# Masked score blocks of a chunked recurrence: one product per level instead of one merged product per half

## The chip, the cores and the metric

The kernel runs on one core of one Trainium2 chip. Its time is the device time of one launch in microseconds. The engines are named as the profile names them: PE is TensorE's matmul row and PEld its weight loads, DVE is VectorE, ACT is ScalarE, POOL is GpSimd and SP is SyncE, whose queue here only issues DMAs.

## The reference

The reference is a two-layer hybrid block followed by one more block of another kind. The change lies in one branch of the two layers, a gated linear recurrence over 512 latent tokens and 256 context tokens, which the reference computes by chunks of 64 tokens, for four heads of width 64 and in two directions (d = 0 forwards, d = 1 backwards):

```python
def step(state, inp):                     # one chunk of 64 tokens
    qc, kc, vc, lf = inp
    a = jnp.cumsum(lf, axis=2)
    ...
    inter = jnp.einsum("bhtk,bhkv->bhtv", qc * jnp.exp(a), state)
    diff = a[:, :, :, None, :] - a[:, :, None, :, :]
    dec = jnp.exp(jnp.where(causal, diff, -jnp.inf))
    scores = jnp.einsum("bhtk,bhsk,bhtsk->bhts", qc, kc, dec)
    intra = jnp.einsum("bhts,bhsv->bhtv", scores, vc)
    return s_new, inter + intra
```

The output of a layer is the sum of both directions. In layer 0 all 768 tokens are computed, in layer 1 the recurrence gives an output for the 512 latent tokens only. Everything else (projections, attention, Fourier mixing, convolution, the second block with its delta rule, cross attention and feed-forward part) is the same before and after.

## The kernel before

Features lie on the 128 partitions, tokens along the free dimension. A projection of layer `ly` is 28 output tiles of 128 features; each tile is summed over eight blocks k of the contraction, and each block takes three fp32r matmuls for a piece of 512 columns (leading part of the weights times leading part of the input, and two products with the remainders) and in layer 0 three more for a piece of 256 columns. `project_split` (L1751) issues them. The first 16 tiles alternate between the two halves of `wide_ps`. From tile 16 on all tiles use half 0 alone, so PE waits at every tile's end until ACT has copied the tile out (L687).

The recurrence runs inside tiles 16 to 27: after each of the 96 blocks of these 12 tiles ("slots" 0 to 95, eight to a tile) `project_split` calls `recurrent_piece(ly, slot)`, which may put a group of small fp32 matmuls into PE's queue. The order of all engines is thus written out by hand. The two head pairs j = 0 and j = 1 come one after the other; the second begins at the slot `SECOND`.

The decay inside a chunk isn't formed. The kernel works by levels l = 0 to 5 with blocks of b = 2^l tokens: at a level the queries of one half of each block of 2b tokens meet the keys of the other half, and between levels DVE multiplies queries and keys by the gates of the block just closed. For each level and direction:

- PE, `scores` (L1892): for each chunk of 128 tokens four matmuls of 64 rows by 64 columns with 32 moving columns, one in each quadrant of the array, from `hg_k` and half of the columns of `hg_q` into `score_bank(d, r)`. Direction 0 has the two banks of `wide_ps[:, 1]`, direction 1 the two of `pair_ps`. That is 24 matmuls in layer 0 (six chunks) and 16 in layer 1 (four); each appears twice in the profile, so a group is 48 or 32 records.
- DVE, `level` (L1210 to L1216): two predicated copies (one for each head of the pair) put the wanted elements of the score banks into one tile `pair_scores`, which the kernel had cleared before (L1367); then one multiplication of the queries (L1213), one of the keys (L1214) and one of the gates (L1216). The two directions write to different elements of `pair_scores`.

The score groups of both directions are issued together, at slots 3, 7, 11, 15, 19 and 23 of the pair. When all twelve are merged, `values` (L1904) multiplies `pair_scores` by the values once, with 64 moving columns, into `pair_ps` (`out_bank`). `keys_by_token` (L1848) turns the keys at slot 26, ACT copies them (L743), `updates` (L1870) forms the state increments of both directions at slot 31, in `duo_ps` and in `wide_ps[:, 1]`, DVE's `states` (L1227, L1231) runs the recurrence over 12 chunks, and `carried` (L1917) adds the part that comes from the states at slot 39. `head_mean` (L1942) sums squares for a head's norm; ACT's `head_root` follows it with a logarithm and an exponential, each set with its own table load, before it copies out the next tile.

With `SECOND = 48` the groups at slots 7, 15, 23, 31, 39, 47, 55, 63, 71, 79, 87 and 95 stand between the last block of a tile and the first of the next.

POOL subtracts the leading part from each weight chunk (L528, 128x1024 elements) soon after ACT has written that part (L700), once for each tile, and multiplies queries and keys for the diagonal (L567, L569).

Of the kernel before, what the change touches and what calls it, by code (L numbers as in the profile page):

```python
# [22 lines left out]
P = 128  # L23
# [119 lines left out]
def build(nc, tokens, mem, positions, weights, const_d, const2_d, par_d, out):  # L143
    with ExitStack() as ctx:
# [44 lines left out]
        pair_scores = proj[:, CV, :].rearrange("p (r t) -> p r t", r=2)  # L189
# [12 lines left out]
        two_banks = lambda d: (wide_ps[:, 1, :], pair_ps[:, :])[d]  # L202
        score_bank = lambda d, r: two_banks(d)[:, 512 * r:512 * r + 512]
        update_ps = lambda d: (duo_ps[:, :], wide_ps[:, 1, :])[d]
# [422 lines left out]
        def _(act):  # L627
# [111 lines left out]
            def keys_by_token(ly, j, d):  # L739

                u = 4 * ly + 2 * j + d
                act.wait_ge(hg_kt_ps, u + 1)
                act.activation(k_tok(d), update_ps(d)[:, 0:TOK].rearrange("p (c f) -> p c f", c=NCH), ACT.Copy).then_inc(hg_kt, 1)  # L743
# [36 lines left out]
            def recurrent_steps(ly, t):  # L780
# [11 lines left out]
                if t == 21:  # L792
                    act.wait_ge(hg_s, 4 * ly + 2)
                    for d in range(2):
                        gates(ly, 1, d)
                if t == 22:
                    values_by_token(ly, 1)
# [3 lines left out]
                if t == 25:  # L801
                    for d in range(2):
                        keys_by_token(ly, 1, d)
                if t == 26:
                    act.wait_ge(sc_used, 2 * ly + 2)
# [322 lines left out]
        def _(dve):  # L1128
# [58 lines left out]
            def level(ly, j, l):  # L1187
# [3 lines left out]
                for d in range(2):  # L1191
# [14 lines left out]
                    mask = cst[f"level{d}"][:, 32 * l:32 * l + 32].bitcast(I32).rearrange("p (n b) -> p n b", b=b)  # L1206
                    mask = mask.unsqueeze(1).broadcast_to([P, len(chunk_list(ly)), HD // (2 * b), b])
                    for r in range(2):
                        mine_of = halves(pair_scores[:, r, 0:2 * cols], b)[:, :, mine, :].rearrange("p (c n) b -> p c n b", c=len(chunk_list(ly)))
                        ins = dve.copy_predicated(mine_of, mask, score_bank(d, r)[:, 0:cols].rearrange("p (c n b) -> p c n b", b=b, n=HD // (2 * b)))  # L1210
# [9 lines left out]
            def states(ly, j, d):  # L1220
# [3 lines left out]
                new = lambda c: update_ps(d)[:, 512 * (c % 2) + 64 * (c // 2):512 * (c % 2) + 64 * (c // 2) + 64]  # L1224
# [132 lines left out]
            for ly in range(DEPTH):  # L1357
# [8 lines left out]
                dve.wait_ge(conv_out, 2 * ly)  # L1366
                link(dve.memset(proj[:, CV, :], 0.0))  # L1367
# [1264 lines left out]
```

## Time and profile before

| | |
|---|---|
| median of 3 runs | 1953.26 us (1952.07 to 1955.52) |
| profiled execution | 1953.26 us, span of the engines 1951.5 us |
| mean granted TensorE clock | 0.964 |
| PE busy, PEld busy | 1766.4 us (91%), 1405.0 us (72%) |
| DVE, ACT, POOL busy | 812.1 us (42%), 717.0 us (37%), 598.2 us (31%) |
| chain that ended last | PE 41%, DVE 7%, ACT 2%, issue 2% of the span |

Busy shares are of the whole span. A busy PE isn't a PE at its peak, since the ends of matmuls are modelled; the distance between the starts of two matmuls tells more than their durations, which contain the way through the array. The granted clock is 1 at full speed (2.4 GHz) and 0.50 at half (1.2 GHz).

### The profile page before, as it was taken

What the parts mean: (1) busy time and instruction counts of PE and PEld (TensorE: products, weight loads), DVE (VectorE), ACT (ScalarE), POOL (GpSimd) and SP (SyncE); (2) the same over time, 40 slices, a digit from 0 to 9 for tenths busy, and PEclk for the clock granted to TensorE, in tenths of its full rate; (3) what the DMA queues carried; (4) which work ended last, traced back from release to release, by engine and by line L of the source; (5) the groups of instructions that cost most, each with busy time, mean ns of one, the idle gap of its engine ahead of it and who ended that gap; (6) DMA issues with size and microseconds to landing.
All of it is one profiled execution on the core that took longest, in us unless ns stands there. A gap on an engine that the chain in (4) does not pass through costs nothing.

```text
span 1951.5 us, 32357 instructions
## 1 busy us (share of the span) xinstructions
PE 1766.4 (91%) x13594; PEld 1405.0 (72%) x13594; DVE 812.1 (42%) x1471; ACT 717.0 (37%) x1115; POOL 598.2 (31%) x318
## 2 busy tenths in 40 slices
PE   6799899978989988989879988888999999999996
PEld 2687788845878766657767766887678678888885
DVE  0301165417350265355656658656424443323112
ACT  3323413226343624254543877003433432222222
POOL 0221312173113323453013411311334334444442
PEclk9899999999999999999899999899999999999998
DMA  8344311130122111311422210000220222222231
GB/s 324 103 158 142 108 35 45 62 113 1 45 86 86 65 56 55 109 44 65 140 99 86 86 55 2 3 3 12 76 76 22 76 76 91 93 98 97 97 107 66
DMA packets 43145, 154.27 MB, mean 79 GB/s; under 512 B 4480, under 2 KB 5632, under 8 KB 42752
## 3 DMA queue, kind: packets, MB, share of 16 engines
q1 hardware_dynamic: 39456, 142.82, 21.2%
q10 hardware_dynamic: 3552, 9.44, 1.3%
q8 instruction: 108, 1.77, 0.4%
q14 instruction: 29, 0.24, 0.0%
HBM read 148.05 MB, written 4.19 MB: 78 GB/s over the span
## 4 chain that ended last, share of the span: by engine, by line
PE 41%; DVE 7%; ACT 2%; issue 2%; DVEq 0%; ACTq 0%
PE wide_ps L1751 29%; PE wide_ps L1772 2%; PE pair_ps L2327 1%; PE wide_ps L2324 1%; PE wide_ps L2303 1%; PE wide_ps L2262 1%; DVE xn L1519 1%; PE duo_ps L2431 1%; PE wide_ps L2412 1%; DVE xn L1669 1%; PE wide_ps L1787 1%; PE pair_ps L1826 1%; DVE ring_r L1170 1%; PE pair_ps L2262 0%; DVE h L1673 0%
## 5 line engine op out<-in xcount | busy, mean ns | idle before, releaser
L528 POOL TENSOR_TENSOR ring_r<-ring,scratch_r 128x1024 fp32r<-128x1024 f32 x179 | 432.2, 2415 | 1082.8 <-ACT scratch_r L700 1054.8
L1751 PE MATMUL wide_ps<-xn_r,scratch_r 128*128 128x512 f32 (+1 forms) x1320 | 490.1, 371 | 0.0
L1751 PE MATMUL wide_ps<-work_r,scratch_r 128*128 128x512 f32 (+1 forms) x1151 | 445.2, 387 | 22.9 <-DVE xn_r L1162 12.0
L700 ACT ACTIVATE scratch_r<-ring 128x1024 fp32r<-128x1024 f32 x195 | 206.7, 1061 | 609.7 <-PE wide_ps L1751 456.8
L1751 PE MATMUL wide_ps<-work_r,ring_r 128*128 128x512 f32 (+1 forms) x1151 | 429.5, 373 | 0.0
L1751 PEld LDWEIGHTS wide_ps<-xn_r,scratch_r 128*128 128x128 f32 x1320 | 252.1, 191 | 49.1 <-issue 5.4
L1751 PEld LDWEIGHTS wide_ps<-work_r,scratch_r 128*128 128x128 f32 x1151 | 218.7, 190 | 75.0 <-issue 18.8
L1751 PEld LDWEIGHTS wide_ps<-work_r,ring_r 128*128 128x128 f32 x1151 | 218.8, 190 | 40.0
L1751 PE MATMUL wide_ps<-proj_r,scratch_r 128*128 128x512 f32 x704 | 238.0, 386 | 1.5 <-DVE proj_r L1162 1.5
L1751 PEld LDWEIGHTS wide_ps<-proj_r,scratch_r 128*128 128x128 f32 x704 | 133.1, 189 | 31.1 <-DVE proj_r L1162 1.9
L687 ACT ACTIVATE proj<-wide_ps 128x512 f32<-128x512 f32 (+2 forms) x116 | 73.8, 636 | 163.8 <-PE wide_ps L1751 154.8
L1267 DVE SCALAR_TENSOR_TENSOR proj<-proj,par_sb,qe 128x768 f32<-128x768 f32 (+1 forms) x6 | 6.2, 1037 | 213.2 <-ACT qe L651 213.2
L1315 DVE TENSOR_TENSOR work<-work 128x512 f32<-128x512 f32 (+2 forms) x35 | 36.4, 1041 | 125.0 <-ACT work L659 124.2
L1751 PE MATMUL wide_ps<-proj_r,ring_r 128*128 128x512 f32 x208 | 82.6, 397 | 0.0
L1751 PE MATMUL wide_ps<-conv_tmp_r,scratch_r 128*128 128x512 f32 (+1 forms) x185 | 69.4, 375 | 0.0
L1751 PE MATMUL wide_ps<-conv_tmp_r,ring_r 128*128 128x512 f32 (+1 forms) x185 | 69.2, 374 | 0.0
L1703 DVE TENSOR_TENSOR proj<-proj,qe 128x512 f32<-128x512 f32 x11 | 27.5, 2501 | 82.2 <-ACT qe L687 82.2
L1703 DVE TENSOR_TENSOR proj<-proj,state 128x512 f32<-128x512 f32 x11 | 27.5, 2500 | 80.5 <-ACT state L687 80.5
L1335 DVE TENSOR_TENSOR h<-h,work 128x768 f32<-128x768 f32 (+1 forms) x16 | 29.8, 1862 | 65.3 <-ACT work L871 65.3
L659 ACT ACTIVATE work<-h 128x512 f32<-128x512 f32 (+2 forms) x56 | 36.2, 660 | 54.2 <-DVE work L1315 16.6
L1751 PEld LDWEIGHTS wide_ps<-proj_r,ring_r 128*128 128x128 f32 x208 | 39.3, 189 | 9.3
L2016 PE MATMUL wide_ps<-proj 64*128 64x256 f32 (+1 forms) x144 | 29.7, 529 | 17.1 <-ACT xn L827 14.5
(392 smaller groups left out, 2906.4 us busy)
## 6 DMA issues: line engine op xcount, KB each, us to landing
ring<-weights SPq DMA_DIRECT2D x260, 512.0 KB, 3.5
h<-tokens SPq DMA_DIRECT2D x4, 768.0 KB, 11.8
h<-tokens ACTq DMA_DIRECT2D x1, 3072.0 KB, 10.0
out<-h ACTq DMA_DIRECT2D x1, 2048.0 KB, 7.3
h<-out ACTq DMA_DIRECT2D x1, 2048.0 KB, 8.6
out<-h SPq DMA_DIRECT2D x8, 256.0 KB, 2.1
const_sb<-const SPq DMA_DIRECT2D x1, 1089.0 KB, 6.3
h<-mem ACTq DMA_DIRECT2D x1, 1024.0 KB, 12.1
```

Source lines behind the costliest of these rows:

```text
L528: pool.tensor_tensor(as_r(wt), wt, as_r(w_lead(m)).bitcast(F32), ALU.subtract).then_inc(w_split, 1)
L659: act.activation(square_sum(n)[:, 0:w] if first else squares(n)[:, k % 2, 0:w], src, ACT.Square).then_inc(sq_ready, 1)
L687: act.activation(dst, wide_ps[0:rows, g % 2 if bank is None else bank, 0:w], func).then_inc(evacuated, 1)
L700: act.activation(as_r(w_lead(m)), ring[:, c % RING, :], ACT.Copy).then_inc(w_lead_ready, 1)
L1170: dve.tensor_tensor(as_r(wt), wt, as_r(w_lead(m)).bitcast(F32), ALU.subtract).then_inc(w_split, 1)
L1315: dve.tensor_tensor(total, total, squares(n)[:, k % 2, 0:w], ALU.add).then_inc(sq_used, 2 if k == 1 else 1)
L1335: dve.tensor_tensor(h[:, n, 0:w], h[:, n, 0:w], resid[:, n % 2, 0:w], ALU.add).then_inc(h_ready, 1)
L1519: link(dve.tensor_tensor_reduce(probs(n)[:, r * (b - a):(r + 1) * (b - a)], win_bank(n, r)[:, 0:b - a], cst2["window"][:, ma:mb], HD ** -0 ...
L1703: dve.tensor_tensor(tile_2[:, t, :], tile_2[:, t, :], up_2[t % 2], ALU.mult).then_inc(ffn_ready, 1)
L1751: last = pe.matmul(wide_ps[:, bank, a:b], wt[:, cols], as_r(x[:, a:b]), start=n == 0 and p == 0, stop=n == len(k_order) - 1 and p == 2)
L1772: last = pe.matmul(ps[:, a:b], wt[:, cols], as_r(x[:, a:b]), start=k == 0 and p == 0, stop=k == KT - 1 and p == 2)
L2016: last = pe.matmul(wide_ps[:, r, a:b], proj[rows, AQ + i, c * CH:(c + 1) * CH], proj[rows, AK, a:b], start=True, stop=True)
```

## The change

The merge is given up. Each level and direction gets its own masked block, and PE multiplies each of them by the values.

- DVE multiplies the score bank by a 0/1 mask (`tensor_tensor`, one operand in PSUM, one in SBUF) into `masked(l, d)`, one of four places in two of the 28 projection tiles, in place of the predicated copy. The clearing of the merged tile goes. Before it writes, DVE waits until the values product of four groups earlier has been done.
- PE's `values` is issued for each level and direction: 12 groups for each pair and layer in place of one, with 32 moving columns, written to every second run of b columns of the output bank.
- Both directions use one pair of score banks, so the scores of one direction wait for the masking of the other's. The output bank is then free for the whole time.
- Both directions' state increments use `duo_ps`; `updates(1)` waits for `states(0)`.
- The slots are laid out anew: scores at 1 and 2, then scores and values in turn at each slot from 4 to 23, the diagonal at 6, keys at 24 and 28, the last values at 25 and 26, updates at 30 and 35, `carried` at 40, and `SECOND` is 46. `head_mean` of the first pair is at slot 60 (before 62) and of the second at 93 (before 95). ACT's copies follow this order.

```diff
-        pair_scores = proj[:, CV, :].rearrange("p (r t) -> p r t", r=2)
+        masked = lambda l, d: proj[:, CV + d, 384 * (l % 2):384 * (l % 2) + 384].rearrange("p (r t) -> p r t", r=2)
...
-        score_bank = lambda d, r: two_banks(d)[:, 512 * r:512 * r + 512]
-        update_ps = lambda d: (duo_ps[:, :], wide_ps[:, 1, :])[d]
+        score_bank = lambda r: wide_ps[:, 1, 512 * r:512 * r + 512]
...
-                    if e > 1:
-                        dve.wait_ge(sc_ready, e - 1)
-                    if l == 0 and d == 0:
-                        dve.wait_ge(sc_used, 2 * ly + j)
+                    if e > 4:
+                        dve.wait_ge(sc_used, e - 4)
...
-                        ins = dve.copy_predicated(mine_of, mask, score_bank(d, r)[:, 0:cols].rearrange("p (c n b) -> p c n b", b=b, n=HD // (2 * b)))
+                        ins = dve.tensor_tensor(masked(l, d)[:, r, 0:cols].rearrange("p (c t) -> p c t", t=32),
+                                                score_bank(r)[:, 0:cols].rearrange("p (c t) -> p c t", t=32), mask, ALU.mult)
...
-                dve.wait_ge(conv_out, 2 * ly)
-                link(dve.memset(proj[:, CV, :], 0.0))
...
             def updates(ly, j, d):
-                pe.wait_ge(hg_kt, u + 1)
+                pe.wait_ge(hg_kt, 4 * ly + 2 * j + 2)
+                if d:
+                    pe.wait_ge(hg_s, u)
...
             def scores(ly, j, l, d):
-                if e > 2:
-                    pe.wait_ge(sc_ready, e - 2)
+                if e > 1:
+                    pe.wait_ge(sc_ready, e - 1)
...
-            def values(ly, j):
-                pe.wait_ge(sc_ready, level_count(ly, j, HG_LEVELS - 1, 1))
+            def values(ly, j, l, d):
+                e = level_count(ly, j, l, d)
+                pe.wait_ge(sc_ready, e)
...
-                            last = pe.matmul(out_bank(a)[rows, 64 * c:64 * c + 64], hg_v[tokens_half, c, rows],
-                                             pair_scores[tokens_half, r, 64 * c:64 * c + 64], start=c == 0, stop=False, skip_group_check=True)
+                            last = pe.matmul(halves(out_bank(a)[rows, 64 * c:64 * c + 64], 1 << l)[:, :, 1 - d, :], hg_v[tokens_half, c, rows],
+                                             masked(l, d)[tokens_half, r, 32 * c:32 * c + 32], start=l == 0 and d == 0 and c == 0,
+                                             stop=False, skip_group_check=True)
...
-            SECOND = 48
+            SECOND = 46
...
-                if slot in (0, SECOND - 1):
+                if n == 0:
                     heads_by_token(ly, j)
-                if 3 <= n < 24 and n % 4 == 3:
-                    for d in range(2):
-                        scores(ly, j, n // 4, d)
+                if n in (1, 2):
+                    scores(ly, j, 0, n - 1)
+                if 4 <= n < 24:
+                    l, step = divmod(n - 4, 4)
+                    d, of_values = divmod(step, 2)
+                    if of_values:
+                        values(ly, j, l, d)
+                    else:
+                        scores(ly, j, l + 1, d)
...
-                if n == 31:
-                    for d in range(2):
-                        updates(ly, j, d)
-                if n == 39:
+                if n == 24:
+                    keys_by_token(ly, j, 0)
+                if n in (25, 26):
+                    values(ly, j, HG_LEVELS - 1, n - 25)
+                if n == 28:
+                    keys_by_token(ly, j, 1)
+                if n in (30, 35):
+                    updates(ly, j, (n - 30) // 5)
+                if n == 40:
                     carried(ly, j)
```

## Rows read from the trace of the kernel before

**Rows 1.** Busy time by stretch: both recurrence stretches, then two pieces at half clock.

```profile
core 0: us, PE busy (x) PEld busy (x) DVE busy (x) ACT busy (x) POOL busy (x), PEclk, DMA share, GB/s
241.00:396.00 155.00, 148.45 (x2252) 128.72 (x2252) 78.92 (x172) 37.32 (x42) 32.53 (x14) 0.97 0.18 63
697.00:816.00 119.00, 104.62 (x1492) 81.38 (x1492) 67.21 (x172) 39.78 (x48) 32.18 (x15) 0.97 0.22 74
346.00:351.80 5.80, 5.80 (x18) 4.93 (x19) 4.18 (x3) 0.95 (x1) 2.37 (x1) 0.50 0.00 0
778.60:781.90 3.30, 3.30 (x9) 2.27 (x7) 0.09 (x1) 0.00 (x0) 2.37 (x1) 0.50 0.00 0
```

**Rows 2.** Waits of PE, whole run: total us, times, longest us.

```profile
PE pair_ps L1892 <- DVE proj L1214: 5.1, 5, 1.5
PE wide_ps L1848 <- DVE proj L1214: 4.5, 4, 1.5
```

**Rows 3.** Waits of PE in the two stretches alone, layer 0 first.

```profile
PE wide_ps L1751 <- ACT proj L687: 4.5, 3, 2.7
...
PE wide_ps L1751 <- ACT proj L687: 6.3, 3, 2.9
```

**Rows 4.** Timeline of PE, layer 0, a pair of score groups (start, duration, what).

```profile
247.93 0.28 PE L1751 MATMUL wide_ps<-work_r,ring_r 128*128 128x256 f32 x1
248.14 0.90 PE L1892 MATMUL wide_ps<-h,proj 64*64 64x32 f32 x48
248.86 0.88 PE L1892 MATMUL pair_ps<-h,proj 64*64 64x32 f32 x48
249.67 0.50 PE L1751 MATMUL wide_ps<-work_r,scratch_r 128*128 128x512 f32 x1
250.01 0.39 PE L1751 MATMUL wide_ps<-xn_r,scratch_r 128*128 128x512 f32 x1
250.24 0.39 PE L1751 MATMUL wide_ps<-work_r,ring_r 128*128 128x512 f32 x1
```

**Rows 5.** Timeline of PE, layer 0, the single group of values.

```profile
287.76 0.28 PE L1751 MATMUL wide_ps<-work_r,ring_r 128*128 128x256 f32 x1
287.97 0.93 PE L1904 MATMUL pair_ps<-proj,h 64*64 64x64 f32 x48
288.83 0.50 PE L1751 MATMUL wide_ps<-work_r,scratch_r 128*128 128x512 f32 x1
```

**Rows 6.** Timeline of PE, layer 1, a pair of score groups.

```profile
757.68 0.40 PE L1751 MATMUL wide_ps<-work_r,ring_r 128*128 128x512 f32 x1
758.01 0.67 PE L1892 MATMUL wide_ps<-h,proj 64*64 64x32 f32 x32
758.50 0.65 PE L1892 MATMUL pair_ps<-h,proj 64*64 64x32 f32 x32
759.07 0.50 PE L1751 MATMUL wide_ps<-work_r,scratch_r 128*128 128x512 f32 x1
```

**Rows 7.** Timelines at tile ends: PE and ACT in layer 0, ACT in layer 1.

```profile
315.07 0.82 PE L1848 MATMUL duo_ps<-const_sb,proj 128*128 128x128 f32 x6
316.13 0.50 PE L1751 MATMUL wide_ps<-work_r,scratch_r 128*128 128x512 f32 x1 [0.24 <-ACT proj L687]
...
315.26 0.81 ACT L687 ACTIVATE proj<-wide_ps 128x768 f32<-128x768 f32 x1 [5.59 <-PE wide_ps L1751]
...
744.39 0.60 ACT L687 ACTIVATE proj<-wide_ps 128x512 f32<-128x512 f32 x1 [5.63 <-PE wide_ps L1751]
```

**Rows 8.** Timelines of DVE and POOL, layer 0: two places where they overlap.

```profile
257.43 2.56 POOL L528 TENSOR_TENSOR ring_r<-ring,scratch_r 128x1024 fp32r<-128x1024 f32 x1 [14.23 <-ACT scratch_r L700]
...
257.65 2.76 DVE L1214 TENSOR_TENSOR proj<-proj,h 128x384 f32<-128x384 f32 x1
...
294.45 3.13 DVE L1231 SCALAR_TENSOR_TENSOR state<-state,h,duo_ps 128x64 f32<-128x64 f32 x10
...
295.28 2.40 POOL L528 TENSOR_TENSOR ring_r<-ring,scratch_r 128x1024 fp32r<-128x1024 f32 x1 [10.72 <-ACT scratch_r L700]
```

**Rows 9.** Busy time in a later stretch of 64x64 matmuls alone, columns as Rows 1.

```profile
1251.00:1290.00 39.00, 39.00 (x1344) 39.00 (x1341) 20.25 (x42) 0.00 (x0) 0.00 (x0) 1.00 0.02 5
```

More of the change, by code:

```diff
@@ L1855, in keys_by_token @@
                 if d:
[L1856 removed]
+                    pe.wait_ge(hg_kt, u)
                 elif j:
@@ L1869, in updates @@
                         for r, rows in enumerate(HALF):
-                            last = pe.matmul(update_ps(d)[rows, 512 * a + 64 * c:512 * a + 64 * c + 64], k_tok(d)[tokens_half, c, rows],
+                            last = pe.matmul(duo_ps[rows, 512 * a + 64 * c:512 * a + 64 * c + 64], k_tok(d)[tokens_half, c, rows],
                                              hg_v[tokens_half, c, rows], start=True, stop=True, skip_group_check=True)
@@ L1891, in scores @@
                         for r, rows in enumerate(HALF):
-                            last = pe.matmul(score_bank(d, r)[tokens_half, 32 * c:32 * c + 32], hg_k(j, d)[rows, chunk_cols(c, a)],
+                            last = pe.matmul(score_bank(r)[tokens_half, 32 * c:32 * c + 32], hg_k(j, d)[rows, chunk_cols(c, a)],
                                              halves(hg_q(d)[rows, chunk_cols(c, a)], 1 << l)[:, :, 1 - d, :], start=True, stop=True,
@@ L1952, in heads_by_token @@
                 by_token(proj[:, HI[j], :], duo_ps, vt_ps)
-            SECOND = 48
+            SECOND = 46
             def recurrent_piece(ly, slot):
-                j, n = (0, slot) if slot < SECOND - 1 else (1, slot - SECOND)
-                if slot in (0, SECOND - 1):
+                j, n = (0, slot) if slot < SECOND else (1, slot - SECOND)
+                if n == 0:
                     heads_by_token(ly, j)
-                if 3 <= n < 24 and n % 4 == 3:
-                    for d in range(2):
-                        scores(ly, j, n // 4, d)
-                if n == 5:
-                    diagonal(ly, j)
-                if n == 26:
-                    for d in range(2):
-                        keys_by_token(ly, j, d)
-                if n == 27:
-                    values(ly, j)
-                if n == 31:
-                    for d in range(2):
-                        updates(ly, j, d)
-                if n == 39:
+                if n in (1, 2):
[7 more added lines that the diff above has]
+                        scores(ly, j, l + 1, d)
+                if n == 6:
+                    diagonal(ly, j)
+                if n == 24:
[7 more added lines that the diff above has]
+                if n == 40:
                     carried(ly, j)
@@ L1977, in recurrent_piece @@
                     head_mean(ly, 0)
-                if slot == 95:
+                if slot == 93:
                     head_mean(ly, 1)
```

28 lines of the change are left out of this document (12 added, 16 removed).

## The prediction

> **What bounds the kernel now.** I read the shares of busy time first, then the waits of PE, then PE's timeline through the two stretches in which the recurrence runs. In those stretches PE is busy for 148.45 of 155 us in layer 0 and for 104.62 of 119 us in layer 1, DVE for 78.92 and 67.21 us [rows 1]. The projection's matmuls follow each other at 0.23 us for 512 columns [rows 4], and half of that, 0.12, for 256. Nothing waits for weights there. So PE's in-order queue is the path: whatever is put into it, and whatever it waits for inside it, moves the end of the layer. A slot of the projection is 3 x (0.23 + 0.12) = 1.05 us in layer 0 and 0.69 us in layer 1.
>
> The waits that the change can touch are few. PE waits 9.6 us for DVE's key multiplications in all [rows 2], and the longest wait for ACT's tile copy is 2.7 us in layer 0 and 2.9 us in layer 1 [rows 3]; that is the tile end at which ACT is still busy with the root of the head norm.
>
> **The change part by part.**
>
> *The groups.* In layer 0 the stream before a pair of score groups would have gone on at 247.93 + 0.12 = 248.05; it goes on at 249.67, and its first matmul takes 0.34 until the next start where 0.23 is usual [rows 4]. A pair costs 1.62 + 0.11 = 1.73 us, of which the second group is 0.72. The single group of values costs 288.83 - 287.88 + 0.11 = 1.06 us [rows 5], although it has 64 moving columns where the scores have 32: the spacing, 0.015 us a record, doesn't depend on the columns here. In layer 1 the pair costs 759.07 - 757.91 + 0.11 = 1.27 us, the second group 0.49 of it [rows 6]; a single one is then 0.78, and 0.83 with the 0.05 by which layer 0's measured single exceeds its own difference.
>
> Before, a pair of heads has six score pairs and one values group. After, it has 24 groups, each in a slot of its own. Layer 0: 24 x 1.06 - 6 x 1.73 - 1.06 = 14.0 us. Layer 1: 24 x 0.83 - 6 x 1.27 - 0.83 = 11.5 us. Twice each, for j = 0 and 1: **+50.9 us**. The value groups that the trace doesn't show (32 columns, written to every second run) I price by the nearest row, the score groups, which read such runs. Lower bound: only the spacing of the 44 more groups, 22 x 0.72 + 22 x 0.49 = 26.6 us. Upper bound: the 64x64 matmuls of the later stretch, half of whose products are written so, which take 39.00 us for 1344 records, 0.029 us each [rows 9]; that stretch uses two quadrants at a time where the recurrence uses four, so I don't take it.
>
> What a change of tile shape costs is 1.73 - 2 x 0.72 = 0.29 us, the part of a pair that isn't its groups [rows 4]; 17 more such changes in each of four halves make 19.7 of the 50.9 us. The Trainium skill, TensorEngine Tiling, Key Properties, says that changing the tiling mode drains the engine. By that rule a regrouping into single slots is what one wouldn't do; without it the sum would be 19.7 us lower. The trace agrees with it.
>
> *Updates and keys apart.* Four pairs of update groups (24 matmuls in both layers) become singles: 2 x 1.06 - 1.73 = 0.39 each; with some 0.1 for each of the four pairs of transposes: **+2.0**.
>
> *Tile ends.* Before, a group stands at each tile's end and hides ACT's copy. How much it hides is seen at 315.07: the stream would have gone on there, the copy runs from 315.26 for 0.81 us, and PE goes on at 316.13 [rows 7], 1.06 us later, 1.17 with the slow first matmul. In layer 1 the copy takes 0.60 [rows 7], so 0.96. After the change nothing stands at slots 31, 39, 79 and 87: 4 x 1.17 + 4 x 0.96 = 8.5 us. At seven other tile ends of each layer a single group of 0.95 or 0.72 covers 1.06 or 0.85: 14 x 0.12 = 1.7. Together **+10.2**. The last `head_mean`, which ran beside the last copy, now stands two slots earlier in the open: at most a single group's price in each layer, 1.06 and 0.83, of which I take 0.75 each: **+1.5**.
>
> *Waits that go.* The scores of the two directions now stand two slots apart, each with its values between: 2 x (1.05 + 1.06) = 4.2 us in layer 0, 2 x (0.69 + 0.83) = 3.0 in layer 1. DVE's whole work in the stretch is 78.92 / 24 = 3.3 and 67.21 / 24 = 2.8 us for each level and direction [rows 1], states and all. So the keys are ready when scores need them, and the 9.6 us of [rows 2] go, with about 1.4 us of half clock behind one of them: the granted clock of 0.97 over 119 us means 7 us at half clock in layer 1, of which 3.3 lie elsewhere [rows 1]. `head_mean` is two slots earlier, which with the groups between gives ACT 3 x 1.05 + 3 x 1.06 = 6.3 us before the tile ends where it had 1.05 + 1.73 + 2.7 = 5.5; in layer 1 3 x 0.69 + 3 x 0.83 = 4.6 where it had 0.69 + 1.27 + 2.9 = 4.9. The wait goes in layer 0 (2.7) and all but some 0.5 in layer 1 (2.4). PE then doesn't stand still, and the half clock after it (0.50 over 5.80 and 3.30 us [rows 1]) gives back 2.9 and 1.6. Sum: 9.6 + 1.4 + 2.7 + 2.4 + 2.9 + 1.6 = **-20.6**.
>
> *Waits that come.* With `SECOND` at 46 the scores of the second pair stand at slots 47 and 48, and in layer 1 the gates (ACT, twice as many operations as in layer 0), POOL's products and DVE's mask of level 0 come later than that. What is late next is DVE: its query multiplication has both operands in SBUF, and such an operation took 2.76 us beside POOL's 2.56 us subtraction [rows 8]. PE's next score group waits for the mask behind it. I take one such wait, 2.8 us, and half clock behind it as in [rows 1], 1.6: **+4.4**. Below, nothing, if POOL happens to be idle; above, the same in layer 0 too, 8.8.
>
> *DVE's own saving* (masking by one multiplication, no clearing) I cost at nothing: DVE stands idle for half of the time [rows 1], and it waits for PE. The new mask operation has one operand in PSUM; DVE's state chain, which has too, ran ten operations in 3.13 us straight through POOL's 2.40 us [rows 8], so POOL doesn't hold it up.
>
> Sum: 50.9 + 2.0 + 10.2 + 1.5 - 20.6 + 4.4 = +48.4 us. The profiled execution took 1953.26 us, which is also the median, around a span of 1951.5. **Forecast: 1953.3 + 48.4 = 2001.7 us.** PE has no later wait for something that isn't shifted with it, so nothing absorbs it.
>
> **The rivals.**
>
> 1. *PE waits for masks.* One pair of banks: each score group waits for the masking of the one before. Against it: the 4.2 and 3.0 us above. For it: POOL holds DVE up by more than 2 us once a tile, and layer 1 has 0.2 us of room by my average. If the 44 score groups after the first of each half waited 0.5 us each, +22: 2024 us.
> 2. *The value groups are slower.* At 0.029 us a record a group is 1.40 us instead of 0.72 in layer 0 and 0.93 instead of 0.49 in layer 1: 24 x 0.68 + 24 x 0.44 = +27, so 2029 us. The Trainium skill, TensorE: Matmul & The Clock Gate, Back-to-back issue gap, gives a floor of about 25 ns from start to start however small the matmul. The 0.015 us of [rows 4] are below it, four quadrants at work, so the trace speaks against it.
> 3. *Cheaper regrouping.* Only the spacing is added (26.6 instead of 50.9), the rest as above: 1977 us. It would need the change of shape to cost nothing when it comes at every slot; [rows 4 to 6] show it each time.
> 4. *Other side, faster.* What PE gets back (20.6 us) outweighs what it is given. Place: the 44 value groups. They would have to cost under 20.6 / 44 = 0.47 us each, all else nothing; even their bare spacing is 0.72 and 0.49. At 0.3 us, with no tile end exposed, 13 - 21 = -8: 1945 us.
>
> **How the numbers follow.** Forecast 0.62, rival 1 0.12, rival 2 0.08, rival 3 0.14, rival 4 0.04. The forecast's own range is 1990 to 2013: the waits that come from nothing to 8.8, and half of the 20.6 not returned. Toward rivals 1 and 3 I widen it to 1982 to 2023, which leaves out rival 2, rival 4 and the outer parts of 1 and 3, under 0.2. A difference of under 0.2%, 4 us, is about what a measurement of this kernel can't tell from none. Slower takes all cases but the fourth: 0.95; same 0.02, faster 0.03.
>
> **What the profile of the changed kernel would show.** PE: 24 single groups for each half, value groups of 48 and 32 records spaced 0.015 us, 1.0 and 0.8 us of the stream each (rivals 2 and 3 fall or stand by this). The two stretches longer by some 26 and 22 us, the rest equal. The waits of PE for DVE's L1214 gone, and the wait of 2.7 us for ACT with its half clock too. Gaps of 1 us at four tile ends of each layer. In layer 1 one wait of PE of 2 to 3 us soon after slot 48. DVE's busy time down. Waits of PE's score groups for the mask line would mean rival 1. The forecast fails if the groups hide beside something I haven't seen, or if the clock falls to half more often than now.

## The result, and the profile after

The change makes the kernel slower: a median of 2006.96 us (2000.58 to 2008.24, 4 runs) against 1954.39 us (1952.07 to 1957.18, 4 runs) for the kernel before on the same chip, a ratio of 1.0262 with a 95% interval of 1.0235 to 1.0288. That is about 51 us; the forecast was 48.4, and 2006.96 lies in its range. The profiled execution took 2004.55 us around a span of 2002.8 us, at a mean granted clock of 0.963.

Busy time over the whole span, from the page of the kernel after:

```profile
PE 1819.8 (91%) x15354; PEld 1436.4 (72%) x15354; DVE 798.4 (40%) x1469; ACT 717.4 (36%) x1115; POOL 597.2 (30%) x318
```

PE has 1760 more records (15354 for 13594), which is 22 x 48 + 22 x 32: the 44 added groups. PE is busy 53 us longer, about as much as the span has grown (51). DVE is busy 14 us less, and nothing of that shows in the time.

Busy time by stretch, columns as in [rows 1]: the two recurrence stretches, then a piece of the second one.

```profile
242.00:424.00 182.00, 173.47 (x3308) 147.43 (x3308) 72.51 (x172) 39.72 (x44) 32.93 (x15) 0.99 0.17 57
725.00:864.00 139.00, 128.27 (x2198) 92.34 (x2197) 65.08 (x173) 39.51 (x47) 31.40 (x16) 0.96 0.21 67
795.40:806.60 11.20, 11.19 (x142) 7.34 (x142) 5.43 (x14) 0.00 (x0) 0.00 (x0) 0.54 0.01 1
```

From the first matmul of tile 16 to the first one behind tile 27 (of the Fourier mixing, so that the wait for the last head norm's root is inside), the stretch of layer 0 goes from 157.4 us (241.51 to 398.95) to 182.2 (242.17 to 424.33), and that of layer 1 from 118.9 (697.32 to 816.23) to 139.0 (724.56 to 863.59). They hold 24.7 and 20.1 us of the 51.3 by which the spans differ. The other 6.5 lie before, between and behind them, 3.9 behind the second, where no instruction was changed.

PE's timeline in layer 0, four slots with one group each, the matmuls of the slots between left out:

```profile
265.58 0.28 PE L1743 MATMUL wide_ps<-conv_tmp_r,ring_r 128*128 128x256 f32 x1
265.79 0.90 PE L1883 MATMUL wide_ps<-h,proj 64*64 64x32 f32 x48
266.62 0.50 PE L1743 MATMUL wide_ps<-work_r,scratch_r 128*128 128x512 f32 x1
266.95 0.39 PE L1743 MATMUL wide_ps<-xn_r,scratch_r 128*128 128x512 f32 x1
...
267.86 0.90 PE L1899 MATMUL pair_ps<-proj,h 64*64 64x32 f32 x48
...
269.93 0.90 PE L1883 MATMUL wide_ps<-h,proj 64*64 64x32 f32 x48
...
272.01 0.90 PE L1899 MATMUL pair_ps<-proj,h 64*64 64x32 f32 x48
```

And in layer 1:

```profile
740.39 0.67 PE L1883 MATMUL wide_ps<-h,proj 64*64 64x32 f32 x32
740.99 0.50 PE L1743 MATMUL wide_ps<-work_r,scratch_r 128*128 128x512 f32 x1
...
741.88 0.67 PE L1899 MATMUL pair_ps<-proj,h 64*64 64x32 f32 x32
```

The starts of neighbouring groups are 2.07 us apart in layer 0. The slot itself is 1.05, so a group costs 1.02 us of the stream. In layer 1 they are 1.49 apart, of which 0.69 is the slot: 0.80 us. Value groups (L1899) and score groups (L1883) have the same length and leave the same gap behind them, although the first write to every second run and have other operands.

Waits of PE over the whole run, where the change touches them (total us, times, longest us):

```profile
PE wide_ps L1743 <- ACT proj L685: 11.0, 12, 1.7
PE pair_ps L2056 <- ACT proj L649: 7.5, 2, 4.1
PE wide_ps L1883 <- DVE proj L1203: 3.3, 3, 2.4
```

The 9.6 us of [rows 2] for the multiplied keys are gone. The waits for ACT's tile copy have the same total as before, 10.8 us in 6 then and 11.0 in 12 now, but they are others: the two long ones of [rows 3] have given way to many of 0.7 to 1.0. This is one of those of layer 0, in the PE timeline and in ACT's:

```profile
305.57 0.50 PE L1743 MATMUL wide_ps<-work_r,scratch_r 128*128 128x512 f32 x1
...
307.78 0.50 PE L1743 MATMUL wide_ps<-work_r,scratch_r 128*128 128x512 f32 x1 [0.90 <-ACT proj L685]
```

```profile
306.92 0.81 ACT L685 ACTIVATE proj<-wide_ps 128x768 f32<-128x768 f32 x1 [3.37 <-PE wide_ps L1743]
```

No group stands between the tile's last block and the next tile's first, so PE waits for the whole copy (in [rows 7] a group lies beside it). The slot takes 2.21 us from start to start, 1.16 more than a bare one, although the profile counts only 0.90 as idle: idle time begins at the modelled end of the last matmul, later than the point at which the next could have started. So the waits of the profile are lower bounds of what they cost. The last kind of wait is new. At the start of the second pair in layer 1, PE's timeline (first fence), DVE's and POOL's:

```profile
790.72 0.67 PE L1883 MATMUL wide_ps<-h,proj 64*64 64x32 f32 x32 [0.39 <-DVE proj L1203]
...
795.41 0.95 PE L1883 MATMUL wide_ps<-h,proj 64*64 64x32 f32 x32 [2.43 <-DVE proj L1203]
796.29 0.79 PE L1743 MATMUL wide_ps<-work_r,scratch_r 128*128 128x512 f32 x1
...
797.87 1.08 PE L1899 MATMUL pair_ps<-proj,h 64*64 64x32 f32 x32
```

```profile
790.49 1.15 DVE L1207 TENSOR_TENSOR h<-h 128x256 f32<-128x256 f32 x1
791.55 2.72 DVE L1208 TENSOR_TENSOR proj<-proj,h 128x384 f32<-128x384 f32 x1
```

```profile
791.31 2.55 POOL L526 TENSOR_TENSOR ring_r<-ring,scratch_r 128x1024 fp32r<-128x1024 f32 x1
```

DVE's multiplication of the keys of level 0, direction 0 takes 2.72 us beside POOL's subtraction, where it takes 0.55 alone (545 to 553 ns in the other 47 cases). The mask of direction 1 stands behind it in DVE's order, and the score group of level 1 waits 2.43 us for that mask. Then PE's matmuls are longer (1.08 us for a group of 32 records, 0.67 elsewhere) for 11.2 us, in which the granted clock is 0.54. What that costs can be read off the same layer's first pair, where the same groups run at full clock:

```profile
730.46 0.67 PE L1883 MATMUL wide_ps<-h,proj 64*64 64x32 f32 x32
...
737.42 0.67 PE L1883 MATMUL wide_ps<-h,proj 64*64 64x32 f32 x32
```

From the score group of level 1, direction 0 to that of level 2, direction 0 it is 6.96 us here, of which some 0.15 are a tile's end that the second pair doesn't have, and 11.26 there (795.41 to 806.67): 4.5 us lost.

### The profile page after: what moved, and what is told of

It is laid out like the page before. It is cut to its first block, busy times and chain, and to the rows that moved or that the text cites. A ratio compares the mean times of both kernels' runs of the same rounds, so it can differ in the third digit from the quotient of the medians.

```text
span 2002.8 us, 35872 instructions
## 1 busy us (share of the span) xinstructions
PE 1819.8 (91%) x15354; PEld 1436.4 (72%) x15354; DVE 798.4 (40%) x1469; ACT 717.4 (36%) x1115; POOL 597.2 (30%) x318
## 4 chain that ended last, share of the span: by engine, by line
PE 40%; DVE 6%; ACT 2%; issue 2%; DVEq 0%; ACTq 0%
PE wide_ps L1743 28%; PE wide_ps L1764 2%; PE pair_ps L2329 1%; PE wide_ps L2326 1%; PE wide_ps L2305 1%; PE wide_ps L2264 1%; DVE xn L1511 1%; PE duo_ps L2433 1%; PE wide_ps L2414 1%; DVE xn L1661 1%; PE wide_ps L1779 1%; PE pair_ps L1818 1%; DVE ring_r L1167 1%; PE pair_ps L2264 0%; DVE h L1665 0%
## 5 line engine op out<-in xcount | busy, mean ns | idle before, releaser
L1743 PE MATMUL wide_ps<-work_r,scratch_r 128*128 128x512 f32 (+1 forms) x1151 | 452.7, 393 | 24.1 <-DVE xn_r L1159 12.2
L1743 PEld LDWEIGHTS wide_ps<-xn_r,scratch_r 128*128 128x128 f32 x1320 | 251.0, 190 | 47.6 <-issue 6.2
L1309 DVE TENSOR_TENSOR work<-work 128x512 f32<-128x512 f32 (+2 forms) x35 | 36.4, 1040 | 125.2 <-ACT work L657 124.3
L1203 DVE TENSOR_TENSOR proj<-wide_ps,const_sb 128x192 f32<-128x192 f32 (+1 forms) x96 | 26.6, 319 | 83.1 <-PE wide_ps L1883 81.7
## 6 DMA issues: line engine op xcount, KB each, us to landing
h<-tokens ACTq DMA_DIRECT2D x1, 3072.0 KB, 10.2
```

Of the source, the lines that this page charges most:

```text
L1203: ins = dve.tensor_tensor(masked(l, d)[:, r, 0:cols].rearrange("p (c t) -> p c t", t=32), score_bank(r)[:, 0:cols].rearrange("p (c t) -> p ...
L1309: dve.tensor_tensor(total, total, squares(n)[:, k % 2, 0:w], ALU.add).then_inc(sq_used, 2 if k == 1 else 1)
L1743: last = pe.matmul(wide_ps[:, bank, a:b], wt[:, cols], as_r(x[:, a:b]), start=n == 0 and p == 0, stop=n == len(k_order) - 1 and p == 2)
```

## The experiments

Nine kernels ran. To read the traces against each other I use one measure besides the time: from the start of the first score group to the start of the last `head_mean` group of a layer. These are 92 slots in the kernels with the second pair at 46 and in before and its variants, and 94 in the three with `SECOND` at 48, from which I take two bare slots (2.10 and 1.38 us). The stretches are from the profiled executions, in us, the ratios from all runs of each kernel.

| kernel | layer 0 | layer 1 | ratio to before, 95% interval |
|---|---|---|---|
| before | 146.1 | 111.4 | 1 |
| after | 170.0 | 130.9 | 1.0262 (1.0235 to 1.0288) |
| no_values | 154.7 | 116.9 | 1.0096 (1.0069 to 1.0124) |
| pairs | 163.0 | 119.2 | 1.0176 (1.0158 to 1.0195) |
| second48 | 170.5 | 125.3 | 1.0228 (1.0202 to 1.0253) |
| tile_ends | 165.3 | 126.6 | 1.0209 (1.0190 to 1.0227) |
| pairs_ends | 157.9 | 116.5 | 1.0102 (1.0078 to 1.0126) |
| mask_twice | 171.7 | 128.3 | 1.0263 (1.0246 to 1.0281) |
| before_single | 147.6 | 111.7 | 1.0021 (1.0007 to 1.0036) |
| before_root | 140.6 | 108.2 | 0.9954 (0.9936 to 0.9972) |
| before_root_keys | 138.6 | 106.5 | 0.9940 (0.9921 to 0.9959) |

### The price of the value groups

```diff
-                    if of_values:
-                        values(ly, j, l, d)
-                    else:
+                    if not of_values:
                         scores(ly, j, l + 1, d)
```

(The waits of DVE and ACT that count value groups are adapted, and the first group that is left starts the accumulation.)

> The changed kernel with the value groups of levels 0 to 4 left out: only the two groups of the last level are issued for each pair and layer, so 10 of 12 value groups and with them most of the product of the scores and the values inside a chunk are not computed. Everything else, the masks, the score groups and the slots, stays. Taken out are 20 groups in layer 0 and 20 in layer 1. Theory (value groups cost what the pair in a slot costs, with a change of shape in each): the slot with one group lasts 1.02 us for a value group in layer 0 and 0.80 in layer 1, so -(20 x 1.02 + 20 x 0.80) = -36 us against the changed kernel, about +15 against the kernel before. Rival A (a group costs only its matmuls at the spacing of the scores, 48 x 0.015 = 0.72 and 32 x 0.015 = 0.48): -(14.4 + 9.6) = -24 us. Rival B (matmuls of a value group are slower, 0.029 us each): about -(20 x 1.4 + 20 x 0.93) = -47 us or more.

Measured: 1971.29 us against 1952.28, a ratio of 1.0096. Against the changed kernel that is 0.0166 of 1952, or 32 us less, between the 36 of the theory and the 24 of rival A; the value groups slower than the scores (rival B) are out. The waits decide between the other two. Some of the value groups stood at tile ends, and without them ACT's copies are exposed there:

```profile
PE wide_ps L1743 <- ACT proj L685: 19.8, 21, 1.8
```

That is 8.8 us more in 9 more waits than in the kernel after. The theory's 36.4 less 8.8 make 27.6, and by the table the two stretches shrank by 15.3 + 14.0 = 29.3; rival A would leave 24 - 8.8 = 15. The cleanest piece is layer 0 up to the first `head_mean`, at full clock in both kernels: 113.2 us after and 101.9 here, for 11 value groups that stand at no tile end, or 1.03 us each. In layer 1 the same piece shrank by 13.2 us, of which 4.5 are the half clock that didn't come: 8.7 / 11 = 0.79. Behind these pieces 4 such groups went in each layer. Layer 0 saved 3.9 us, again about the full price; layer 1 only 0.9, because there the wait for ACT's copy behind the head norm's root grew from 0.37 to 1.76 us, and some 1.6 us went to half clock behind it (0.96 over 41 us). So a value group costs a full slot's price, shape changes included. What my expectation forgot is that a group at a tile's end costs nearly nothing, because it lies beside the copy: the slot there takes 2.21 us with the group and 2.22 without it.

### The price of a slot of its own

```diff
                     if of_values:
+                        scores(ly, j, l + 1, d)
                         values(ly, j, l, d)
-                    else:
-                        scores(ly, j, l + 1, d)
...
-                if n in (25, 26):
-                    values(ly, j, HG_LEVELS - 1, n - 25)
+                if n == 26:
+                    for d in range(2):
+                        values(ly, j, HG_LEVELS - 1, d)
```

> The changed kernel with the score group and the value group of one direction issued in the same slot, one behind the other, instead of in neighbouring slots, and the last two value groups together. No matmul is added or left out; what goes are slots with a lone group, 11 for each pair and layer, so 44 in all. Theory (each slot with a group costs one change of shape there and back, 0.29 us by the rows before): -(44 x 0.29) = -13 us against the changed kernel. Rival (the matmuls alone cost, the change of shape nothing): within 2 us of the changed kernel. A third outcome, slower: the score group comes one slot later for the masks, and if the masks were the bound PE waits for them longer; the waits of the line of the values for VectorE would then grow from 0 to several us.

Measured: 1987.80 us, a ratio of 1.0176: 0.0086 or 17 us less than the changed kernel, with the same matmuls. PE's timeline in layer 0:

```profile
265.92 0.90 PE L1883 MATMUL wide_ps<-h,proj 64*64 64x32 f32 x48
266.64 0.88 PE L1899 MATMUL pair_ps<-proj,h 64*64 64x32 f32 x48
267.45 0.50 PE L1743 MATMUL wide_ps<-work_r,scratch_r 128*128 128x512 f32 x1
...
269.73 0.90 PE L1883 MATMUL wide_ps<-h,proj 64*64 64x32 f32 x48
```

Two slots with a pair in one of them take 3.81 us, where after takes 2 x 2.07 = 4.14: 0.33 us for each of the 44 slots freed, 14 to 15 us. The rest isn't a change of shape. The wait at the start of the second pair in layer 1 is 1.76 us instead of 2.43, and the ten microseconds behind it run at full clock:

```profile
785.03 0.67 PE L1883 MATMUL wide_ps<-h,proj 64*64 64x32 f32 x32 [1.76 <-DVE proj L1203]
```

```profile
780.00:790.00 10.00, 7.92 (x179) 6.04 (x180) 8.63 (x17) 1.81 (x3) 3.48 (x2) 1.00 0.06 23
790.00:800.00 10.00, 10.00 (x218) 7.30 (x216) 8.45 (x19) 2.24 (x3) 2.39 (x1) 1.00 0.19 57
```

That is why layer 1 gained 11.7 us and layer 0, which had no half clock there, 7.0: 0.33 x 22 = 7.3 in each, and in layer 1 the 4.5 us of half clock on top. The rival, that the shape change is free, is refuted.

The same cost can be put on the kernel before alone, with nothing else of the change:

```diff
-                if 3 <= n < 24 and n % 4 == 3:
-                    for d in range(2):
-                        scores(ly, j, n // 4, d)
+                if 3 <= n <= 24 and n % 4 in (3, 0):
+                    scores(ly, j, (n - 3) // 4, (n + 1) % 4)
```

> The kernel before with one thing alone: its two score groups of a level, one for each direction, are issued in neighbouring slots (3 and 4, 7 and 8, to 23 and 24) instead of both in slot 3, 7, to 23. No matmul, mask or copy is added. There are 24 more slots with a group between projection slots. Theory (each such slot costs a change of shape there and back of 0.29 us beside its matmuls): +7 us. If the change of shape costs what pairing gained in the changed kernel (17 us for 44 slots, 0.38 each): +9. Rival (a change of shape is free, and pairing gained by something else, such as masks that no longer make PE wait): within 2 us of before.

Measured: 1958.46 us against 1953.96, a ratio of 1.0021 (1.0007 to 1.0036), so +4.1 us where 7 to 9 were expected. The price was as expected; a gain was left out. A score group and its slot take 2.07 us here too (264.63 to 266.70), 24 x 0.33 = +8. But the second direction's scores now come one slot later, and the waits for the keys, 9.6 us in [rows 2], are down to

```profile
PE wide_ps L1848 <- DVE proj L1214: 2.6, 4, 1.0
PE wide_ps L1892 <- DVE proj L1214: 0.3, 1, 0.3
```

or 2.9 us. 8 - 6.7 = +1.3, and the stretches grew by 1.5 + 0.3. The waits for ACT's copy took 1.1 us more (11.9 for 10.8); the rest of the 4.1 isn't placed, and the interval (1.4 to 7.0 us) leaves it open. The runs' times alone wouldn't refute the rival here, but the slots of 2.07 us do. Much of what is paid for more slots is given back by waits, which is what also happens in the change itself, on a larger scale.

### The late masks and the open tile ends

```diff
-            SECOND = 46
+            SECOND = 48
...
-                if slot == SECOND + 14:
+                if slot == SECOND + 12:
                     head_mean(ly, 0)
-                if slot == 93:
+                if slot == 95:
                     head_mean(ly, 1)
```

(ACT's copies of the values and keys follow, in the order that they had before.)

> The changed kernel with the second pair two slots later (slot 48 instead of 46), and the order of ScalarE's copies and the two head_mean slots moved with it. Nothing else moves. Theory: the second pair's first scores waited 2.43 + 0.39 us in layer 1 and 0.46 in layer 0 for the first masks, behind the multiplications of the first pair's close, and some 10 us at half clock followed in layer 1, in which groups lasted 1.08 instead of 0.67; two more slots of projection give the masks 2 to 3 us: -3 us of waits and -3 to -5 of the half clock, together -5 to -8 us against the changed kernel. Rival: the close of the first pair is itself bound to the slots and moves along, so the wait stays: within 2 us. Against: the last group and carried come two slots later and the head_mean of the second pair at slot 95 could be exposed at the end of the layer: up to +2 us.

Measured: 1997.14 us, a ratio of 1.0228: 0.0034 or 7 us less than the changed kernel, within the expected 5 to 8, though the two intervals overlap. The trace shows the place. Layer 1 is 5.6 us shorter and layer 0 isn't (+0.5). The wait for the mask is one of 0.96 us, and the clock stays whole over the ten microseconds behind it:

```profile
PE wide_ps L1884 <- DVE proj L1204: 1.0, 1, 1.0
```

```profile
798.00:808.00 10.00, 9.91 (x231) 6.70 (x223) 7.57 (x18) 1.66 (x2) 2.38 (x1) 1.00 0.19 56
```

The next one adds to it the groups at the tile ends:

```diff
-                j, n = (0, slot) if slot < SECOND else (1, slot - SECOND)
-                if n == 0:
+                j, n = (0, slot) if slot < SECOND - 1 else (1, slot - SECOND)
+                if slot in (0, SECOND - 1):
                     heads_by_token(ly, j)
...
-                if n in (30, 35):
-                    updates(ly, j, (n - 30) // 5)
-                if n == 40:
+                if n in (31, 35):
+                    updates(ly, j, (n - 31) // 4)
+                if n == 39:
                     carried(ly, j)
```

> As the kernel with the second pair at slot 48, and beside it the groups that the change moved off the ends of the tiles put back there: the heads at slot 47, the updates at slots 31 and 35 of each pair, the carried product at slot 39. Theory: PE's wait for ScalarE's copy at the end of a tile (0.90 to 0.96 us four times in layer 0, 0.69 to 0.75 four times in layer 1, 6.6 us together) is covered by these groups: -5 to -7 us against the kernel with the second pair at slot 48 alone, -10 to -15 against the changed kernel. Rival: these groups wait at the tile's end for their own inputs (the states, the copied keys) as long as they were to cover: within 2 us of the kernel with slot 48 alone.

Measured: 1994.40 us, a ratio of 1.0209: 0.0019 or 4 us less than with slot 48 alone, where 5 to 7 were expected (the two intervals overlap widely), and 10 less than the changed kernel. The waits for the copy are halved, as expected (12.4 us in 13 with slot 48 alone):

```profile
PE wide_ps L1744 <- ACT proj L685: 5.6, 5, 1.7
PE wide_ps L1884 <- DVE proj L1204: 1.6, 1, 1.6
PE duo_ps L1865 <- DVE state L1226: 1.2, 2, 0.6
```

Of these 6.8 us layer 0 kept 5.2, and layer 1 lost 1.3. There two small waits came (the second direction's updates for the states, 0.6 each), and the mask wait grew from 0.96 to 1.61 us with half clock behind it, which slot 48 alone didn't have:

```profile
790.00:800.00 10.00, 10.00 (x153) 6.46 (x154) 5.40 (x14) 1.66 (x2) 0.18 (x1) 0.66 0.09 20
```

That is up to (1 - 0.66) x 10 = 3.4 us. Both together with the pairs:

> The changed kernel with both rearrangements in one: the groups in pairs (ratio to before 1.0176 instead of 1.0262 alone) and the second pair at slot 48 with heads, updates and carried at the tile ends (1.0209 alone). Theory: the two are independent terms, the shape changes and the exposed copies with the late masks, so their gains add: 1.0262 - 0.0086 - 0.0053 = 1.0123, about +24 us on before. Rival: they share a part (both give the masks of the second pair more time), then about 1.015, +29 us. That it reaches the kernel before is excluded by both: 48 value groups instead of 4 remain.

Measured: 1974.14 us, a ratio of 1.0102 (1.0078 to 1.0126). The sum of the parts, 1.0123, is inside the interval, and the 1.015 of the rival isn't. In both stretches the granted clock is 1.00 now. So 31 of the 51 us were the layout of the change and not its idea. The 20 that remain (18.7 in the spans) are bought with 44 more groups, whose bare spacing alone is 26.6 us, and paid down by the waits that went.

### How near the masks are to the bound

```diff
-                    for r in range(2):
+                    for n, r in enumerate((0, 1, 0, 1)):
                         ins = dve.tensor_tensor(masked(l, d)[:, r, 0:cols]...
+                        if n == 1:
+                            link(ins)
```

> The changed kernel with the two mask multiplications of each level and direction issued twice, the second time behind the end of the first; the values are the same. It adds 96 operations of 0.32 us (26 to 31 us of VectorE's time, in the middle of the loop scores, mask, values). Theory (VectorE's work is hidden with room to spare: 2.5 us of idle time before the mask of each direction in layer 0, 1.3 us in layer 1 where the multiplications were not slowed): nothing in layer 0, at most some 2 to 4 us in layer 1 at the places where the gated multiplication took 1.74 us instead of 0.41: ratio to before 1.026 to 1.029. Rival (the masks are next to the bound, as in my first rival): +0.55 us for each of 24 masks in layer 1 and some in layer 0, +13 to +26 us, ratio 1.033 to 1.04.

Measured: 2002.79 us against 1949.33, a ratio of 1.0263, where the changed kernel has 1.0262. DVE is busy 825.0 us instead of 798.4, the mask line 53.2 instead of 26.6, and PE's waits for it are

```profile
PE wide_ps L1885 <- DVE proj L1203: 5.0, 6, 1.7
```

5.0 us instead of 3.3. Rival 1 of the prediction, 0.5 us for each of 44 groups, is out: six groups wait, at the start of a pair or beside one of POOL's operations. That the time came out the same is in part luck. The other mask waits grew by some 3 us in all, but the long one of layer 1 was 1.06 us instead of 2.43 and no half clock followed it (0.99 over the 128 us of that layer, where the kernel after has 0.96). A cheaper mask could win at most the 3.3 us of waits and the half clock behind them.

### What the change won, without the change

```diff
-                if t == 23:
+                if t == 24:
                     head_root(ly, 0)
...
-                        if j and l == 3:
+                        if j and l == 4:
                             hgrn_close(ly, 0)
```

> The kernel before with ScalarE's head_root of the first pair one tile later and with the close of the first pair on VectorE behind level 4 instead of level 3. Nothing else moves. Theory: the two long waits of the projection's matmuls for ScalarE's copy (2.7 and 2.9 us), behind head_root, go, and with them the stretch at half clock that follows each: -5.6 and -2 to -5, together -8 to -10 us against before. These are terms that the change won and that can be had without it. Rival: the close, later, holds up the masks of the second pair's level 5 or its product, and what is won is lost there: within 2 us. If the waits only move to the next copy: no change.

(The second part moves DVE's close of the first pair one level later, behind which the root now stands; what that part does alone wasn't run.)

Measured: 1946.87 us against 1953.96, a ratio of 0.9954 (0.9936 to 0.9972), so 9 us faster, as expected. ACT's timeline in the kernel before, at the tile end of 345, and in this one:

```profile
340.66 1.28 ACT L640 ACT_TABLE_LOAD   x1 [10.96 <-PE duo_ps L1942]
341.96 0.90 ACT L650 ACTIVATE proj<-duo_ps,eps 128x768 f32<-128x768 f32 x1
342.89 0.84 ACT L651 ACTIVATE proj<-proj 128x768 f32<-128x768 f32 x1
343.75 1.28 ACT L687 ACT_TABLE_LOAD   x1
345.05 0.81 ACT L687 ACTIVATE proj<-wide_ps 128x768 f32<-128x768 f32 x1
```

```profile
346.47 0.81 ACT L687 ACTIVATE proj<-wide_ps 128x768 f32<-128x768 f32 x1 [12.02 <-PE wide_ps L1751]
...
348.39 1.28 ACT L640 ACT_TABLE_LOAD   x1
```

Before, the copy waits behind 4.3 us of root work and table loads (one load ahead of the logarithm, none between it and the exponential, one ahead of the copy). Here it comes first, and the root follows. Over the six microseconds from 346, the granted clock is 1.00, where [rows 1] had 0.50.

```diff
-                if n == 26:
-                    for d in range(2):
-                        keys_by_token(ly, j, d)
+                if n in (26, 28):
+                    keys_by_token(ly, j, (n - 26) // 2)
```

> As the one before it, and beside it the by-token groups of the keys of the two directions in slots 26 and 28 instead of both in 26, before the masks of the last level are done. Theory: PE's waits for VectorE's keys (four of 2.2 to 4.5 us on before, 9.6 us together, some with half clock after them) come from the group in slot 26 of the second direction, which needs the last level's keys; two slots later (2.9 us of projection) takes most of it: -4 to -7 us against the version with head_root alone, -12 to -16 against before. Rival: what waits is the first direction's group or the value group, which stay where they are: within 2 us of the version with head_root alone.

Measured: 1942.50 us against 1953.96, a ratio of 0.9940 (0.9921 to 0.9959), some 12 us faster than before and the best kernel here. The step over the root alone is 3 us by the ratios, which the intervals don't separate from none, and 3.6 by the stretches. The row L1848 <- L1214 (4.5 us with the root alone) has gone from the list, as expected; what remains is

```profile
PE pair_ps L1892 <- DVE proj L1214: 6.1, 6, 1.5
```

the score groups of the second direction, which this edit doesn't touch. My expectation counted part of them to the by-token groups, hence 3 to 4 instead of 4 to 7, and it misread the trace: the 9.6 us are nine waits of at most 1.5, not four of 2.2 to 4.5.

## Why the prediction was right

I set each term beside the two traces, slot by slot: from the start of a slot's first projection matmul to that of the next, less a bare slot (1.05 and 0.69 us). This counts a wait at what it delays, which is more than the idle time that the profile gives it.

*The groups (+50.9).* Right in kind, 3 us too high. A lone group costs 1.02 and 0.80 us of the stream, not 1.06 and 0.83: 2 x (24 x 1.02 - 6 x 1.73 - 1.06) + 2 x (24 x 0.80 - 6 x 1.27 - 0.80) = 47.6 with before's pairs as in [rows 4, 6]. The shape change was put at 0.29 us; freeing 44 slots gave 0.33 each in the trace. That the value groups would cost what the score groups cost, the unshown price, is confirmed by their spacing and by leaving 40 of them out. The Trainium skill, TensorEngine Tiling, Key Properties, has the engine drain when the tiling mode changes; pairs and before_single agree with it, at a third of a microsecond for there and back.

*Updates and keys apart (+2.0).* 1.5: the updates cost 1.05 us each where a pair cost 1.74; the keys' part can't be told from nothing.

*Tile ends (+10.2).* Right. The four open ends of each layer cost 4.7 and 3.9 us, 8.6 where 8.5 was forecast (2.21 instead of 1.05 us for the slot before 307.78), and a lone group at another tile's end 0.14 more than elsewhere, where 0.12 was forecast. tile_ends took 6.8 us of waits away.

*Waits that go (-20.6).* The first mis-sized term: right in kind, 4 us too small. The waits for the keys went as forecast, but they had cost 11.4 us of the stream and not 9.6, and the half clock behind one of them 1.5 (forecast 1.4, although its own working gives (7 - 3.3) / 2 = 1.9). Behind the root 6.0 us went where 2.7 + 2.4 were forecast, with 4.3 of half clock for 4.5; in layer 1 a wait of 0.37 stays of the 2.87. And 1.6 us went that the forecast doesn't have, at the tile end of slot 47, where a single group lay beside the copy and in layer 1 ACT was late:

```profile
755.03 0.50 PE L1751 MATMUL wide_ps<-work_r,scratch_r 128*128 128x512 f32 x1 [1.68 <-ACT proj L687]
```

In the kernel after, this wait is 0.83 (at 789.36). Together 24.8.

*Waits that come (+4.4).* The second mis-sized term. The place, the cause and the length were right: soon after slot 48 in layer 1, the score group behind the mask, which stands behind a multiplication that POOL's subtraction stretched to 2.72 us; it waited 2.43 us, with 0.39 for the mask before and 0.46 in layer 0. These cost 3.5 us where 2.8 was forecast. The half clock behind was taken as 1.6 us and was 4.5. Together 8.0, near the upper bound of 8.8. second48 shows the cause: with the wait down to 0.96 us, layer 1 loses 5.6 us.

*The last `head_mean` (+1.5).* 1.4. From the start of slot 93 to the first matmul behind tile 27 it is 8.68 us for 7.88 in layer 0 and 6.56 for 5.98 in layer 1. This holds the 1.3 us by which PE waits longer for ACT's root (7.5 for 6.2); with `head_mean` back at slot 95 it is 6.2 again.

*DVE's saving at nothing.* Right as far as the runs tell: 27 us more work on DVE left the time where it was.

*The sum.* 47.6 + 1.5 + 10.3 - 24.8 + 8.0 + 1.4 = 44.0, and 44.8 measured in the two stretches (24.7 and 20.1, where 26 and 22 were forecast). The forecast's 48.4 lies within 4 us of that partly by luck: its two mis-sized terms, each off by about 4 us, cancel. That the whole is 51 and not 45 comes from the 6.5 us outside of the stretches, which the forecast doesn't have. For them no cause was found, and they need not be an effect: from the last `head_mean` of layer 1 to the end, after took 1145.0 us and mask_twice, with the same layout, 1140.7; before, whose last `head_mean` stands two slots later, took 1139.1. So a span of one execution says nothing of differences below some 4 us, and the two stretches are the better measure. The range, too, was not what its text adds up to: waits that come of 0 to 8.8 and half of the 20.6 not returned give 1997 to 2016, not 1990 to 2013.

The rivals. Masks as the bound: mask_twice says no. Slower value groups: the spacing and no_values say no. In that rival the prediction set 0.015 us against a floor for a matmul, but 0.015 is the mean for a record, and two records make a matmul, 0.029 us. The comparison wasn't of like with like; the price of the groups, read from the rows, doesn't hang on it. Cheaper regrouping: pairs says no, the shape change is paid. Faster: the value groups would have had to cost under 0.47 us, and cost 0.80 to 1.02.

## What to carry to other kernels

On an in-order queue that is full, small groups of matmuls of another tile shape cost by the slot as well as by the matmul: put what can stand together into one slot, and put it where the queue would wait anyway. Before waits are bought back with more work, see whether moving an instruction does it: here ACT's root a tile later (with DVE's close of the pair) and PE's second key group two slots later gave 12 us without a matmul more. And price a wait with the clock behind it: the wait of 2.4 us cost another 4.5. Count a term by what it shifts in the stream, not by the idle time that the profile gives it: eight open tile ends were 6.5 us of waits and cost 8.6.

## What the runs showed of the hardware

- Granted clock behind a gap. PE stood still for 2.43 us in the kernel after and then ran 11.2 us at a mean of 0.54, 4.5 us longer than the same groups at full clock; before, 2.70 us were followed by 5.8 at 0.50. Behind 1.76 us in pairs the clock stayed at 1.00, but behind 1.61 us in tile_ends, with another of 1.68 some 7 us earlier, it was 0.66 over 10 us. In the kernel before, two waits of 1.50 us stand at the same place of the two pairs of layer 1: behind the first the clock is 0.70 over 5.6 us (712.6 to 718.2), behind the second 1.00 over 5 us (769.7 to 774.7). The length of one gap alone doesn't order these, and what does isn't settled here.
- Matmuls of 64 rows by 64 columns in all four quadrants leave a record every 0.015 us in the mean, two records a matmul, in groups of 48 and 32, whether they stream 32 columns or 64, and whether they write runs or every second run. In the trace the records come by fours, 7 ns apart, and each four starts 58 ns after the last.
- POOL and DVE. A multiplication on DVE with both operands in SBUF took 2.72 us beside POOL's subtraction of 2.55 and 0.55 alone. The mask multiplication, whose one operand is in PSUM, took 0.32 us in the mean over 96, and 0.28 to 0.36 in the 18 of them that began beside an operation of POOL. The Trainium skill, SBUF — State Buffer, SBUF: two separate sides, says that the two engines share a pair of ports by an exclusive lock, which a DVE operation with two SBUF inputs takes against a GpSimd operation that reads SBUF; these rows agree with it.
